# Reordering one core's encoder step: input turned tile by tile, and ScalarE's squares and high parts put behind its weight step

## What is computed

```python
for layer in range(2):
    xp = rms_norm(hp, g[0])                       # the same for the sample frames hs
    if layer == 0:                                # A: gated MLP, B: windowed attention
        z = xp @ w_in                             # 1024 -> u 512 | va 512 | q 512 | k 128 | v 128
        u, va = gelu(z_u), layer_norm(gelu(z_va))
        mp = concat(u * spatial_mix(va), attention(rope(q), rope(k), v)) @ w_out
    else:                                         # C: trailing means over 2/4/8/16 frames
        mp = (pooled(xp) @ c_w) * c_scale
    hp = hp + rms_norm(mp, g[1])
    h2 = rms_norm(hp, g[2])
    hp = hp + rms_norm((silu(h2 @ w_gate) * (h2 @ w_up)) @ w_out, g[3])     # inner width 2816
```

## Time and the profile before

| | us |
|---|---|
| median of three runs | 1091.4 (1090.87 to 1092.74) |
| the profiled execution | 1087.63 |
| its span | 1085.3 |
| PE busy | 1045.7 (96%) |
| PE weight loads busy | 1019.9 (94%) |
| DVE busy | 623.3 (57%) |
| ACT busy | 511.4 (47%) |
| DMA | 162.5 MB, 150 GB/s mean |

### The profile page before, as it was taken

The page is one execution under the profiler, slowest core; times in us unless marked ns, Lnnn a source line. Parts: engine busy times, 40 slices in busy tenths (PEclk is TensorE's granted clock), DMA queues, the critical chain, the costliest instruction groups (busy, mean ns, idle before and its releaser), DMA issues.

```text
span 1085.3 us, 19346 instructions
## 1 busy us (share of the span) xinstructions
PE 1045.7 (96%) x8087; PEld 1019.9 (94%) x8087; DVE 623.3 (57%) x920; ACT 511.4 (47%) x837; POOL 50.8 (5%) x52
## 2 busy tenths in 40 slices
PE   6999999899999999999989889999999999999997
PEld 4798889899999999999989889999999999999996
DVE  4377855777555545544456666667754545454543
ACT  5531355556444444445456445564544444444542
POOL 0070220000000000000000000200000000000000
PEclk9999999999999999999999999999999999999998
DMA  7413113456665555546654465454565555466552
GB/s 244 98 44 103 40 40 97 138 155 195 195 190 170 165 166 165 159 140 188 179 154 129 132 186 165 129 166 133 164 198 161 170 158 164 145 182 179 152 169 82
DMA packets 307636, 162.47 MB, mean 150 GB/s; under 512 B 14553, under 2 KB 304321, under 8 KB 307550
## 3 DMA queue, kind: packets, MB, share of 16 engines
q1 hardware_dynamic: 305678, 159.11, 50.3%
q10 hardware_dynamic: 1648, 1.78, 0.5%
q0 software_dynamic: 224, 0.35, 0.1%
HBM read 158.63 MB, written 2.58 MB: 149 GB/s over the span
## 4 chain that ended last, share of the span: by engine, by line
PE 78%; DVE 10%; issue 6%; ACT 3%; DMA 1%; POOL 1%; SPq 0%; ACTq 0%; DVEq 0%; POOLq 0%
PE ps L529 25%; PE ps L530 24%; PE ps L531 24%; DVE wlo L1435 3%; ACT whi L1049 2%; DVE tmp L1701 1%; DVE h L1705 1%; PE ps L569 1%; DMA x_tok<-in_x_sample_dram 1%; POOL rs L1946 1%; DVE acc L1687 1%; PE ps L786 1%; PE ps L946 0%; DVE tmp L1715 0%; PE ps L918 0%
## 5 line engine op out<-in xcount | busy, mean ns | idle before, releaser
L1435 DVE TENSOR_TENSOR wlo<-raw,whi 128x1024 fp32r<-128x1024 f32 (+2 forms) x332 | 369.0, 1112 | 309.1 <-ACT whi L1049 308.4
L529 PE MATMUL ps<-xhi,whi 128*128 128x288 f32 (+1 forms) x1600 | 466.5, 292 | 8.7 <-DVE wlo L1435 6.5
L530 PE MATMUL ps<-xlo,whi 128*128 128x288 f32 (+1 forms) x1600 | 462.9, 289 | 0.0
L531 PE MATMUL ps<-xhi,wlo 128*128 128x288 f32 (+1 forms) x1600 | 460.5, 288 | 0.0
L1049 ACT ACTIVATE whi<-raw 128x1024 fp32r<-128x1024 f32 (+2 forms) x332 | 315.1, 953 | 222.2 <-PE ps L531 191.2
L529 PEld LDWEIGHTS ps<-xhi,whi 128*128 128x128 f32 x1600 | 302.4, 189 | 12.2 <-DVE wlo L1435 7.4
L531 PEld LDWEIGHTS ps<-xhi,wlo 128*128 128x128 f32 x1600 | 302.8, 189 | 0.0
L530 PEld LDWEIGHTS ps<-xlo,whi 128*128 128x128 f32 x1600 | 302.6, 189 | 0.0
L529 PE MATMUL ps<-mhi_b,whi 128*128 128x288 f32 x352 | 105.7, 300 | 5.5 <-DVE wlo L1435 5.5
L531 PE MATMUL ps<-mhi_b,wlo 128*128 128x288 f32 x352 | 104.3, 296 | 0.0
L530 PE MATMUL ps<-mlo_b,whi 128*128 128x288 f32 x352 | 102.7, 292 | 0.0
(11 more groups left out here) (216 smaller groups left out, 944.8 us busy)
## 6 DMA issues: line engine op xcount, KB each, us to landing
raw<-in_ffn_w_in_dram SPq DMA_DIRECT2D x176, 512.0 KB, 3.9
raw<-in_ffn_w_out_dram SPq DMA_DIRECT2D x64, 384.0 KB, 3.5
raw<-in_ffn_w_out_dram SPq DMA_DIRECT2D x64, 320.0 KB, 3.1
raw<-in_ab_w_in_dram SPq DMA_DIRECT2D x10, 512.0 KB, 4.0
raw<-in_ab_w_out_dram SPq DMA_DIRECT2D x10, 256.0 KB, 2.8
raw<-in_ab_w_out_dram SPq DMA_DIRECT2D x20, 128.0 KB, 3.1
x_tok<-in_x_prompt_dram SPq DMA_DIRECT2D x4, 512.0 KB, 5.2
raw<-in_ab_w_in_dram SPq DMA_DIRECT2D x8, 256.0 KB, 3.5
```

What stands on the lines that cost most here:

```text
L529: pe.matmul(out, wh, xh, start=first, stop=False)
L530: pe.matmul(out, wh, xl, start=False, stop=False)
L531: return pe.matmul(out, wl, xh, start=False, stop=last)
L1435: dve.tensor_tensor(wlo[:, s, 0:n], raw[:, m % NRAW, 0:n], whi[:, s, 0:n].bitcast(F32), ALU.subtract)\
```

## The change

Four edits.

**1. The start goes by tiles of frames.** PE transposes a tile's eight feature blocks into two banks, DVE scales each half from PSUM by the gains into `tmp` or `tmp2`, ACT makes `xhi` of it and DVE `xlo`; ACT copies the unscaled half to `h` afterwards. The first tile and the first two weight units are loaded first. The products go in 20 blocks of six matmuls by (tile, unit) in the order of `FIRST_BLOCKS`, and tiles 2, 3 and 4 are turned between blocks. Squares and gelu go between ACT's other steps by tile. Eight loads are issued by SP instead of ACT, behind the first weights. ACT loads its function table ahead of the gains (`warm`), and PE does four filler matmuls between two turns.

**2. ACT's order in a slot.** `square_pair` and `x_high` are yielded at slot + 0.5, and the passes call `run(slot + LATER)` after `hi_part(m + 4)`.

**3. The table.** Slots of (0, 1), (1, 1) and (2, 1) move later by one to four, the two units of mixer C in `ffn_in(1, 0)` stand after units 22 and 24 instead of 19 and 21, and DVE's last `x_low` has a slot of its own.

**4. `after_mixer_ab`.** Squares go behind the weight step on ACT; on DVE `lo_part` 9, 10 and 11 move behind the fold of the squares.

```diff
-C_AFTER = ((15, 16), (19, 21))
+C_AFTER = ((15, 16), (22, 24))
-    (1, 1): {"sum": 1, "spread": 2, "scale": (2, 3, 5, 6), "fold": 8, "pre": 10, "rows": (8, 9, 9, 12, 12, 13),
...
+    (1, 1): {"sum": 2, "spread": 4, "scale": (4, 5, 7, 8), "fold": 10, "pre": 12, "rows": (10, 11, 11, 15, 15, 16),
...
-    (2, 1): {"sum": 25, "spread": 26, "scale": (26, 27, 29, 30), "fold": 32, "pre": 34, "again": 35,
-             "x": (35, 36, 38, 39)},
+    (2, 1): {"sum": 28, "spread": 30, "scale": (30, 31, 33, 34), "fold": 36, "pre": 38, "again": 40,
+             "x": (40, 41, 42, 43)},
...
+FIRST_BLOCKS = (*((t, j) for t in range(3) for j in range(2)), *((t, 2) for t in range(3)), *((3, j) for j in range(3)),
+                *((t, 3) for t in range(4)), *((4, j) for j in range(4)))
+TURN_BEFORE = {(1, 0): 2, (0, 2): 3, (0, 3): 4}
...
@@ PE, the start @@
+            def turn_first(t):
+                t0, n = TILES[t]
+                pe.wait_ge(x_loaded[t], 16)
+                for i in range(2):
+                    if t >= 2:
+                        pe.wait_ge(first_scaled, 2 * (t - 2) + i + 1)
+                        pe.wait_ge(first_kept, 2 * (t - 2) + i + 1)
+                    for k in range(4):
+                        c = (4 * i + k) * P
+                        mm = pe.transpose(flat(FIRST_BANKS[t][i], k * P, n), x_tok[0:n, t, c:c + P], ident[0:n, 0:n])
+                    mm.then_inc(first_turned, 1)
...
+            turn_first(0)
+            pe.wait_ge(gains_loaded, 32)
+            pe.transpose(flat(7, 0, 72), gain_rows[:, :], ident[0:72, 0:72]).then_inc(gains_turned, 1)
+            fill(4, 2)
+            turn_first(1)
+            for t, j in FIRST_BLOCKS:
+                if (t, j) in TURN_BEFORE:
+                    turn_first(TURN_BEFORE[t, j])
+                va_block(t, j)
...
@@ DVE, the start @@
+            def scale_first(t, i):
...
+                dve.wait_ge(first_turned, 2 * t + i + 1)
...
+                dve.tensor_tensor(first_x(t, i), first_half(t, i),
+                                  gains[:, 4 * i:4 * i + 4].unsqueeze(2).broadcast_to([P, 4, n]), ALU.mult)\
+                    .then_inc(first_scaled, 1)
...
+            scale_first(0, 0)
+            scale_first(0, 1)
+            lo_part(0)
+            low_first(0, 0)
+            lo_part(1)
+            low_first(0, 1)
...
@@ ACT: norms @@
                 for p, slot in enumerate(at["scale"]):
-                    yield slot
+                    yield slot + LATER
                     square_pair(s, b, p)
...
                 for p, slot in enumerate(at["x"]):
-                    yield slot
+                    yield slot + LATER
                     x_high(s // 2, b, p)
...
@@ ACT: each pass @@
                     run(slot)
                     hi_part(m + 4)
+                    run(slot + LATER)
...
@@ DVE: after_mixer_ab @@
                 add_z(0, 1, 2)
                 residual_pair(0, 0, 1)
                 lo_part(U_OUT + 8)
+                residual_pair(0, 0, 2)
                 add_z(0, 1, 3)
-                residual_pair(0, 0, 2)
-                lo_part(U_OUT + 9)
                 residual_pair(0, 0, 3)
-                add_z(0, 1, 4)
-                lo_part(U_OUT + 10)
                 add_square(0, 0, 3)
                 fold_squares(0, 0)
+                add_z(0, 1, 4)
+                lo_part(U_OUT + 9)
+                invert(0, 0, 1)
                 add_z(0, 1, 5)
-                lo_part(U_OUT + 11)
-                invert(0, 0, 1)
+                lo_part(U_OUT + 10)
                 dve.wait_ge(r_kept[0], KEPT[0, 1])
                 x_scale(0, 0, 0)
+                lo_part(U_OUT + 11)
+                x_low(0, 0, 0)
                 x_scale(0, 0, 1)
                 add_z(0, 1, 6)
-                x_low(0, 0, 0)
```

More of the change, by code:

```diff
@@ L190, in stepper @@
     return run
-LAST = 1 << 20
+LAST, LATER = 1 << 20, 0.5
 def shape_constants():
@@ L557, in _, with va_block @@
             pe.wait_ge(ident_loaded, 16)
[L558 to L576, removed]
+            def turn_first(t):
+                t0, n = TILES[t]
+                pe.wait_ge(x_loaded[t], 16)
[7 more added lines that the diff above has]
+                    mm.then_inc(first_turned, 1)
+            def va_block(t, j):
+                t0, n = TILES[t]
                 m = U_IN + j
@@ L1071, in _ @@
[L1071 to L1075, removed]
             act.wait_ge(set_up, 1)
+            warm(ACT.Copy)
@@ L1092, in _, with high_first, keep_first_rows @@
-            for t, (t0, n) in enumerate(TILES):
-                act.wait_ge(x_loaded[t], 16)
+            def high_first(t, i):
+                act.wait_ge(first_scaled, 2 * t + i + 1)
+                act.activation(first_cols(xhi, t, i), first_x(t, i), ACT.Copy).then_inc(first_hi, 1)
+            def keep_first_rows(t):
+                for i in range(2):
+                    act.wait_ge(first_turned, 2 * t + i + 1)
+                    act.activation(first_cols(h, t, i), first_half(t, i), ACT.Copy).then_inc(first_kept, 1)
@@ L1097, in _, with gelu @@
                                accum_out=ssq[0:n, t:t + 1]).then_inc(x_squared, 1)
-                if t in (0, 3):
-                    hi_part(2 + t // 3)
-            root_first()
+            hi_part(0)
+            high_first(0, 0)
+            hi_part(1)
+            high_first(0, 1)
+            keep_first_rows(0)
+            high_first(1, 0)
+            high_first(1, 1)
+            keep_first_rows(1)
+            high_first(2, 0)
+            high_first(2, 1)
+            hi_part(2)
+            keep_first_rows(2)
+            square_first(0)
+            high_first(3, 0)
+            high_first(3, 1)
+            hi_part(3)
+            keep_first_rows(3)
+            square_first(1)
+            high_first(4, 0)
+            high_first(4, 1)
+            keep_first_rows(4)
+            for t in range(2, NT):
+                square_first(t)
+            root_first()
+            act.wait_ge(first_rstd, 1)
+            def gelu(t):
+                n = TILES[t][1]
+                if t < NT - 1:
+                    act.wait_ge(va_done, t + 1)
+                else:
+                    act.wait_ge(w_used, 4)
+                act.activation(va[0:n, t, :], flat(t, 0, AW, n), ACT.Gelu_apprx_tanh, scale=rstd[0:n, t:t + 1])\
+                    .then_inc(va_gelu, 1)
+            for t in range(3):
+                gelu(t)
             hi_part(4)
-            act.wait_ge(first_rstd, 1)
+            gelu(3)
             hi_part(5)
             hi_part(6)
[L1106 to L1109, removed]
+            gelu(4)
             keep_first()
```

112 lines of the change are left out of this document (66 added, 46 removed).

## The result

The changed kernel takes 1055.7 us (median of four runs, 1054.37 to 1056.61) against 1091.1 us for the kernel before (four runs, 1089.12 to 1092.74): a ratio of 0.9675, interval 0.9655 to 0.9696. The profiled execution took 1054.37 us with a span of 1052.1, so the two profiles differ by 33.2 us. PE is now busy for 1030.7 us (98%).

The account below looks back on a forecast made before the run. PE was taken to bound the kernel, busy 1045.7 of 1085.3 us. The start's 6.2 plus the slots' 16.3 less 0.6 for `after_mixer_ab` gave 21.9 us less, 1091.4 to 1069.5 us; range 1064 to 1081, own range 1065 to 1074.

Parts of the forecast that it names:

- The slots' sum: Feed-forward slots, edits 2 and 3: waits, slow matmuls and power or fold waits removed, 16.3 us less in all.
- I take 10.8: Slots between 538 and 770 us: PE's seven waits for `lo_part`, 12.0 us shown, go; 10.8 us less, bounds 4 and 12.0.
- + 1.5: Slots, behind the wait ending at 632 us: 20 slow matmuls regain full pace, 1.5 us less.
- 4.0: Slots and fold of (0, 1): PE's waits for GpSimd's power and the folded squares go, 4.0 of 4.9 us.
- The start: Start, edit 1: products begin 8.7 us earlier, less 2.5 for turns between them; 6.2 us less, bounds 2.5 to 7.5.
- I let the slow stretch be as long as before: First products of the start: the slow pace, 0.44 us each, was taken to last 4.83 us as before.
- `after_mixer_ab`: Edit 4, between mixer AB and the first feed-forward: 0.6 us more, bounds 0.5 less to 1.5 more.
- The low end: Whole kernel: all bounds at their best give 26.4 us less, 1065.0 us; the range was set from 1064.
- Next wait in the slots: Slots: ACT's loads or later squares become the next wait, half of 16.3 us comes, 1077.7 us; chance 0.20.
- Late clock: Start: turns among products hold the clock low until the last turn, 15.0 us lost, 1084.5 us; chance 0.10.
- Slower: Slots: later squares or `x_high` hold up DVE's queue at 27 places, 13.5 us more, 1099.3 us; chance 0.06.
- Nothing: Whole kernel: mixer AB gives back the start's gain and the slots only shift their waits, 1091 us; chance 0.04.

Follow-up runs that it names:

- e2: The changed kernel with edits 3 and 4 undone, so the start by tiles and ACT's order in a slot: 1057.6 us, ratio 0.9698.
- e9: The kernel before with edit 2 alone, ACT's order in a slot (seven lines): 1065.8 us, ratio 0.9759.
- e7: The changed kernel with ten short PE waits (1.23 us each) added in `ffn_in(0, 1)`, where PE never waits: 1071.1 us, ratio 0.9825.
- e5: The changed kernel without the four filler matmuls between the turns of tiles 0 and 1: 1058.5 us, ratio 0.9706.
- e6: The kernel before with four filler matmuls ahead of its last five transposes: 1088.5 us, ratio 0.9991.
- e8: The changed kernel with ten long PE waits (2.28 us each) added in `ffn_in(0, 1)`: 1093.7 us, ratio 1.003.
- e10: The changed kernel with edits 3 and 4 undone and `x_high` ahead of the weight step again, only the squares behind it: 1062.4 us, ratio 0.9731.
- e1: The changed kernel with edits 2, 3 and 4 undone, so the start by tiles alone: 1080.2 us, ratio 0.9899.
- e4: The changed kernel with edit 4 alone undone, `after_mixer_ab` as before: 1056.3 us, ratio 0.9678.
- e3: The changed kernel with edits 2 and 4 undone, so the start by tiles and the new table: 1080.8 us, ratio 0.9906.

## Why the prediction was wrong

Direction and mechanism held: the slots' waits for `lo_part` came from ACT's order, and all seven went (e2, e9). What failed is the price of a wait. The time failed by 1069.5 - 1055.7 = 13.8 us, in three steps.

**The slots' sum, 16.3 forecast, 25.0 in the profiles.** This is the step that failed: "I do not take the full 12.0 ... I take 10.8", "+ 1.5" for the clock and "4.0" for the power. The terms for the waits and the clock were undersized, and one was missing.
- All of the shown idle time went, 15.4 us in the stretch of the earlier trace rows and about 1.7 in (0, 1), 17.1 against the 14.8 that I took. The loads that I held 1.2 back for made no wait. But 1.7 of the 17.1 are the long power wait that only this one execution had.
- The hidden part was missing altogether. I took a wait for the idle time in brackets; e7 prices it at 0.25 us more. Of 13 waits that is 3.2 us.
- Of slow matmuls I counted those after 632 us. There was a second such stretch, and its window stood open to be read: a stretch's mean clock of 0.99 was the hint, and I did not look for where it was. It stands where the one of e5 stands, behind the pooling of the sample frames (here at 693.54), and no wait is near.

```profile
697.00:700.40 3.40, 3.40 (x18) 3.40 (x18) 1.71 (x2) 1.07 (x2) 0.00 (x0) 0.51 0.01 1
```

  That is 1.4 more, 2.9 with the first. Sum: 17.1 + 3.2 + 2.9 = 23.2 of 25.0. The other 1.8 us I can't put down to rows. The second stretch is luck between two profiles and no work of the change: five of the twelve traces have it (before, e5, e6, e8, e10), and e5 has the changed kernel's slots.
- The pair e1 and e2 holds the order alone, and no such luck. From the first feed-forward to the tail their profiles differ by 21.8 us. The shown waits differ by 13.5 and number 11 fewer, 2.8 us hidden. Three waits of e1 (1.94, 2.76 and 1.73 us) have a slow stretch behind them, 4.5. Together 20.8: the waits cost half as much again as they show.

The split between the edits was off too. I gave 4.0 to the power and the fold, as work of the table. The table is worth 1.3 with the order (e2, e4) and nothing measurable without it (e1, e3). The longest power wait went without table and order (e1, e6); why it was long in the one execution that I read stays open.

**The start, 6.2 forecast, 8.6 measured.** The first product came at 10.68 (forecast 10.9), and the turns cost what I took: from 10.68 to 41.15 is 30.5 us, 27.8 of it for 120 products at 0.2315, 2.7 for the turns (forecast 2.5). The failing sentence is "I let the slow stretch be as long as before". I had the fillers in front of me and gave them no effect; e5 shows that here they end it before the first product, e6 that elsewhere they shorten it. My bounds left that case out: without a slow stretch the same sum is 8.5.

**From profile to median, 2.4 us.** I left the distance of 3.8 us between the profiled run and the median as it was. After, it is 1.4. Such a distance is chance: e6, with the same slots, was profiled 3.1 us above its median. In the sessions of e1 to e8 the kernel before scatters from 1083.8 to 1094.3 over thirty runs, and e1 from 1074.9 to 1082.7, e2 only from 1057.3 to 1058.9. That slow stretches follow the same wait in some executions and not in others fits this (the 1.9 us wait near 557 us: none in the kernel before, one in e1, e3 and e6), but no run tests it, and e8, with ten long waits, scatters by 3.2 us only. The prediction's 0.2% for telling a difference was too fine: the interval of e1 is 0.3% to either side.

**What held.** `after_mixer_ab` costs 0.45 (forecast 0.6), with the fold's wait at 0.8 after 1.3, though the two waits for `x_low` are 0.8 each, not over 1. The low end: all my bounds at their best gave 1065.0. With the hidden part (3.2), the second slow stretch (1.4), a start without one (8.6 for 7.5, 1.1) and the distance (2.4) they would have reached 1056.9.

**The rivals.** *Next wait in the slots* (0.20): no such wait of PE. DVE still waits 10.1 us for ACT's high parts in the stretch shown, but the lead of four units covers it. *Late clock* (0.10): wrong in sign here. Turns among products hold nothing down: in e5 the pace rises at 14.9 us and stays up through the turn at 15.9. *Slower* (0.06): in the slots from 527 to 617 us DVE has no idle time ahead of the additions of squares that its residuals need (other additions wait for ACT 6.4 us in all, 4.3 before, which does not reach PE):

```profile
L1773 DVE TENSOR_TENSOR acc<-acc,tmp 128x512 f32<-128x512 f32 x6 | 4.1, 686 | 0.0
```
*Nothing* (0.04): PE's waits in mixer AB are those of before, and the start's gain passes through (e1).

## What to carry to other kernels

Where one engine prepares operands for a bottleneck engine and also does side work that waits for a third, put the preparing step first in each slot: a wait that stands in front of it delays everything downstream by a slot, and seven lines that swap the two were worth 26 us of 1091. When such waits are summed from a trace, add to each the part hidden in drawn-out matmuls (0.25 us here), read the clock behind each of over 1.5 us, and look for slow windows without a wait as well. Read more than one execution before a single long wait or slow stretch goes into a sum. Test what an edit is worth with and without its neighbours: the table showed nothing alone and 1.3 us behind the order.

## What the runs showed of the hardware

- A pause of PE of 2.28 us in a dense stream was followed by 3.7 us at half pace nine times in ten (e8), one of 1.23 us never in ten (e7). The slots of the kernel before, e1, e3, e6 and e10 agree: of their waits for `lo_part` and the power, none of the twelve of 1.0 to 1.3 us was followed by a slow stretch, 7 of the 13 of 1.7 to 2.5 us were, and all six of 2.7 to 2.9 us. In the mixer one wait of 1.33 us was, in e9, where seven other traces have the same wait without. What decides between 1.7 and 2.5 us stays open.
- The pace also fell without a pause. In five of the twelve traces it did so 2 to 4 us after the start of the pooling of the sample frames, 16 matmul records of 32 columns in 1.97 us, during which PE counts as busy.
- The granted clock shows this slow pace (0.51 to 0.66 in these windows), but not that of the start, where it reads 1.00 with products 0.44 us apart (e5's window above, and the earlier trace rows). At the start only the spacing of the matmuls tells.
- GpSimd's subtraction of 128x544 took 1.09 us in e7 and e8, while its multiplication of the same shape takes 1.50 in the mixer (three in 4.49). I had priced the one by the other. It is not the multiplication as such: another one there, of 128x512 by a broadcast operand, takes 1.04 (L1934). The reason was not looked for.
